# Decay products of a two-block layer kernel in one pass over stacked high and low parts, with their loads after x

## The reference

```python
h = rmsnorm(x, norm_mix[l])
proj = h @ w_in[l]
q, k, v, r, lr_f, lr_b, u, g_a, g_b = jnp.split(proj, split_points, axis=-1)
log_a_f = log_sigmoid(lr_f @ w_decay_up_fwd[l] + b_decay_fwd[l]) / 16
log_a_b = log_sigmoid(lr_b @ w_decay_up_bwd[l] + b_decay_bwd[l]) / 16
...
b = jnp.cumsum(log_a, axis=chunk)     # inside gla_chunked, chunks of 64 tokens
```

## Time and profile before

| | us |
|---|---|
| median of 3 runs | 1387.95 (1386.64 to 1388.97) |
| the profiled execution, its own time | 1387.89 |
| its span, from the first instruction to the last | 1385.6 |
| PE busy | 1334.7 (96% of the span) |
| DVE, ACT, POOL busy | 742.9, 574.2, 517.9 |
| mean granted TensorE clock | 0.992 of full speed |

### The profile page before, as it was taken

The page is one execution under the profiler, slowest core; times in us unless marked ns, Lnnn a source line. Parts: engine busy times, 40 slices in busy tenths (PEclk is TensorE's granted clock), DMA queues, the critical chain, the costliest instruction groups (busy, mean ns, idle before and its releaser), DMA issues.

```text
span 1385.6 us, 21045 instructions
## 1 busy us (share of the span) xinstructions
PE 1334.7 (96%) x8106; PEld 1093.6 (79%) x8106; DVE 742.9 (54%) x1226; ACT 574.2 (41%) x776; POOL 517.9 (37%) x130
## 2 busy tenths in 40 slices
PE   6999999999999999999999989999999999999997
PEld 4878889778887888888887867777878878787885
DVE  4642450664556888888822252334667777302553
ACT  6544353443343222222232245555554565533233
POOL 5332423333333333344344412323443343334331
PEclk9999999999999999999999999999999999999998
DMA  6232312215234455555423433231223222223221
GB/s 186 65 106 68 91 46 75 91 48 182 91 92 112 133 147 146 142 142 138 114 84 87 120 92 91 76 106 49 74 61 86 65 61 74 79 91 98 85 91 61
DMA packets 201731, 133.22 MB, mean 96 GB/s; under 512 B 4599, under 2 KB 197864, under 8 KB 201686
## 3 DMA queue, kind: packets, MB, share of 16 engines
q1 hardware_dynamic: 200390, 130.29, 32.1%
q10 hardware_dynamic: 848, 1.60, 0.4%
q0 software_dynamic: 448, 0.71, 0.2%
HBM read 130.46 MB, written 2.12 MB: 96 GB/s over the span
## 4 chain that ended last, share of the span: by engine, by line
issue 66%; POOL 16%; PE 15%; ACT 1%; DVE 1%; DMA 1%; POOLq 0%; SPq 0%; ACTq 0%
POOL wlo L447 15%; PE acc L469 4%; PE acc L471 4%; PE acc L470 4%; PE acc L1791 1%; PE acc L1793 1%; PE acc L1792 1%; DMA xnat<-in_x_dram 1%; ACT whi L443 0%; ACT hhi L692 0%; PE mid L2237 0%; POOLq L1764 0%; DVE hw L1607 0%; DVE wlo L1506 0%; DVE hw L1608 0%
## 5 line engine op out<-in xcount | busy, mean ns | idle before, releaser
L447 POOL TENSOR_TENSOR wlo<-raw,whi 128x2048 fp32r<-128x2048 f32 (+1 forms) x109 | 504.9, 4632 | 829.4 <-ACT whi L443 829.4
L469 PE MATMUL acc<-hhi,whi 128*128 128x512 f32 x1104 | 441.7, 400 | 4.4 <-DVE hq L1573 2.1
L471 PE MATMUL acc<-hhi,wlo 128*128 128x512 f32 x1104 | 431.5, 391 | 0.0
L470 PE MATMUL acc<-hlo,whi 128*128 128x512 f32 x1104 | 431.4, 391 | 0.0
L469 PEld LDWEIGHTS acc<-hhi,whi 128*128 128x128 f32 x1104 | 208.1, 188 | 51.1 <-issue 7.9
L470 PEld LDWEIGHTS acc<-hlo,whi 128*128 128x128 f32 x1104 | 208.2, 189 | 44.8 <-issue 3.4
L471 PEld LDWEIGHTS acc<-hhi,wlo 128*128 128x128 f32 x1104 | 208.0, 188 | 44.2
L443 ACT ACTIVATE whi<-raw 128x2048 fp32r<-128x2048 f32 (+1 forms) x110 | 203.5, 1850 | 48.7 <-PE acc L471 42.7
L1433 DVE TENSOR_TENSOR ada<-ada 128x512 f32<-128x512 f32 x24 | 108.9, 4538 | 0.8
L469 PE MATMUL acc<-ahi,whi 128*128 128x512 f32 x176 | 69.5, 395 | 1.8 <-POOL wlo L447 1.5
L875 ACT ACTIVATE fsg<-fsg 128x512 f32<-128x512 f32 x22 | 13.9, 632 | 138.2 <-DVE fsg L1447 138.1
(11 more groups left out here) (375 smaller groups left out, 2058.6 us busy)
## 6 DMA issues: line engine op xcount, KB each, us to landing
raw<-in_w_in_dram SPq DMA_DIRECT2D x56, 512.0 KB
raw<-in_w_in_dram SPq DMA_DIRECT2D x26, 1024.0 KB
raw<-in_w_ffn_in_dram SPq DMA_DIRECT2D x44, 512.0 KB
ada<-in_w_ada_dram SPq DMA_DIRECT2D x24, 512.0 KB, 3.8
raw<-in_w_ffn_out_dram SPq DMA_DIRECT2D x16, 704.0 KB
raw<-in_w_out_dram SPq DMA_DIRECT2D x8, 1024.0 KB
xnat<-in_x_dram SPq DMA_DIRECT2D x8, 512.0 KB, 7.1
raw<-in_w_branch_gla_dram SPq DMA_DIRECT2D x4, 1024.0 KB
```

Source lines behind the costliest of these rows:

```text
L447: nc.gpsimd.tensor_tensor(wlo[:, slot, 0:n], raw[:, slot, 0:n], whi[:, slot, 0:n].bitcast(f32), ALU.subtract).then_inc(s_unit_lo, 1)
L469: nc.tensor.matmul(acc[bank][:, :], h, xh[:, k, :], start=(k == 0), stop=False)
L470: nc.tensor.matmul(acc[bank][:, :], h, xl[:, k, :], start=False, stop=False)
L471: last = nc.tensor.matmul(acc[bank][:, :], lo, xh[:, k, :], start=False, stop=(k == nk - 1))
```

## The change

The four strips of `lrT` are summed and spread over all strips by one float32 product with a constant 0/1 matrix (`lr_sum`, a new input of 64 KB, loaded by SP behind `wlr`) into the bank M[0]. ACT copies that, rounded, to `lr3`; on strip 1 DVE replaces the copy by the low part (M[0] minus the rounded value). POOL copies `wup` rounded to `wup3` and replaces strip 2 by the low part of the weights; strip 3 of the weights stays zero, and only three copies of the up weights are loaded. One fp32r product of `wup3` with `lr3` then adds high x high (strip 0), high weights x low lr (strip 1) and low weights x high lr (strip 2). The eight decay products use it in place of the float32 product.

On POOL the wait for the last quarter of x moves ahead of all its loads, and the up weights come first, then `relb` and `hot`, the masks and `edge`; behind them stand a wait for the six loads and the two preparing operations, and only then `split_lo` of unit 1.

```diff
+    strip_sum = np.tile(np.eye(LR, dtype=f), (P // LR, P // LR))
...
             sp.dma_start(wlr[:, :, :], kview(w_in, C_LR, LR)).then_inc(s_lr_in, 16)
+            sp.dma_start(lr_sum[:, :], inp["strip_sum"]).then_inc(s_lr_in, 16)
...
             A(lrT[:, :], acc[b][:, :], ACT.Copy).then_inc(s_acc_free[b], 1)
+            act.wait_ge(s_lr3, 1)
+            A(lr3[:, :], M[0][:, :], ACT.Copy).then_inc(s_lr3, 1)
             act.wait_ge(s_col_mm, 2)
...
+            dve.wait_ge(s_lr3, 2)
+            V.tensor_tensor(lr3[LR:2 * LR, :], M[0][LR:2 * LR, :], lr3[LR:2 * LR, :].bitcast(f32), ALU.subtract)\
+                .then_inc(s_lr3, 1)
             dve.wait_ge(s_cols, 2)
...
+            pool.wait_ge(s_pool_prep, 3)
+            pool.wait_ge(s_x_in[TT - 1], 16)
+            for c in range(3):
+                pool.dma_start(wup[c * LR:c * LR + RANK, 0, :], inp["w_decay_up_fwd"][0]).then_inc(s_wup_in, 16)
+                pool.dma_start(wup[c * LR + RANK:(c + 1) * LR, 1, :], inp["w_decay_up_bwd"][0]).then_inc(s_wup_in, 16)
             pool.dma_start(relb[0:N_BUCKETS, :], inp["rel_bias_2"]).then_inc(s_bias_src, 16)
             pool.dma_start(hot[:, :], inp["hot"]).then_inc(s_bias_src, 16)
-            for c in range(P // LR):
-                pool.dma_start(wup[c * LR:c * LR + RANK, 0, :], inp["w_decay_up_fwd"][0]).then_inc(s_wup_in, 16)
-                pool.dma_start(wup[c * LR + RANK:(c + 1) * LR, 1, :], inp["w_decay_up_bwd"][0]).then_inc(s_wup_in, 16)
-            pool.wait_ge(s_x_in[TT - 1], 16)
...
+            pool.wait_ge(s_wup_in, 6 * 16)
+            nc.gpsimd.tensor_copy(wup3[:, :, :], wup[:, :, :]).then_inc(s_pool_prep, 1)
+            pool.wait_ge(s_pool_prep, 4)
+            lows = slice(2 * LR, 3 * LR)
+            nc.gpsimd.tensor_tensor(wup3[lows, :, :], wup[lows, :, :], wup3[lows, :, :].bitcast(f32), ALU.subtract)\
+                .then_inc(s_pool_prep, 1)
+            pool.wait_ge(s_pool_prep, 5)
             split_lo(pool, 1, 0)
...
             last.then_inc(s_acc_full, 1)
+            pe.wait_ge(*moved(U_LR, 0))
+            mm(M[0][:, :], lr_sum[:, :], lrT[:, :], start=True, stop=True).then_inc(s_lr3, 1)
             pe.wait_ge(s_rows_in, 12 * 16)
...
-            pe.wait_ge(*moved(U_LR, 0))
-            pe.wait_ge(s_wup_in, 2 * (P // LR) * 16)
+            pe.wait_ge(s_pool_prep, 5)
+            pe.wait_ge(s_lr3, 3)
...
-                mm(M[i % 4][:, :], wup[:, i // 4, (i % 4) * P:(i % 4 + 1) * P], lrT[:, :], start=True, stop=True)\
+                mm(M[i % 4][:, :], wup3[:, i // 4, (i % 4) * P:(i % 4 + 1) * P], lr3[:, :], start=True, stop=True)\
```

More of the change, by code:

```diff
@@ L108, in shape_constants @@
     hot[N_BUCKETS] = np.where(count > 0, np.log(np.maximum(count, 1)), NEG_INF)
-    return {"ident": ident, "masks": masks, "edge": edge, "hot": hot}
+    strip_sum = np.tile(np.eye(LR, dtype=f), (P // LR, P // LR))
+    return {"strip_sum": strip_sum, "ident": ident, "masks": masks, "edge": edge, "hot": hot}
 def build(nc, inp, out):
@@ L174, in build @@
     lrT = at("lrT", A0 + 44, [P, L])
+    lr_sum = at("lr_sum", A0 + 59, [P, P])
+    lr3 = at("lr3", A0 + 60, [P, L], f32r)
+    wup3 = at("wup3", A0 + 62, [P, 2, L], f32r)
     gq, gk = at("gq", A0 + 32, [P, L]), at("gk", A0 + 34, [P, L])
@@ L341, in build @@
         s_lr_in = sem("lr_in")
+        s_lr3 = sem("lr3")
         s_mask_src = sem("mask_src")
@@ L383, in build @@
         s_upad_zero = sem("upad_zero")
-        s_vrow_zero = sem("vrow_zero")
+        s_pool_prep = sem("pool_prep")
         s_wup_in = sem("wup_in")
@@ L557, in _ @@
             sp.dma_start(wlr[:, :, :], kview(w_in, C_LR, LR)).then_inc(s_lr_in, 16)
-            sp.wait_ge(s_vrow_zero, 3)
+            sp.dma_start(lr_sum[:, :], inp["strip_sum"]).then_inc(s_lr_in, 16)
+            sp.wait_ge(s_pool_prep, 3)
             for name, r in ROWS:
@@ L1734, in _ @@
         def _(pool):
[L1735 to L1739, removed]
+            nc.gpsimd.memset(vrow[:, :], 0.0).then_inc(s_pool_prep, 1)
+            nc.gpsimd.memset(wup[:, :, :], 0.0).then_inc(s_pool_prep, 1)
+            nc.gpsimd.memset(relb[:, :], 1.0).then_inc(s_pool_prep, 1)
+            pool.wait_ge(s_pool_prep, 3)
[3 more added lines that the diff above has]
+                pool.dma_start(wup[c * LR + RANK:(c + 1) * LR, 1, :], inp["w_decay_up_bwd"][0]).then_inc(s_wup_in, 16)
             pool.dma_start(relb[0:N_BUCKETS, :], inp["rel_bias_2"]).then_inc(s_bias_src, 16)
             pool.dma_start(hot[:, :], inp["hot"]).then_inc(s_bias_src, 16)
-            for c in range(P // LR):
-                pool.dma_start(wup[c * LR:c * LR + RANK, 0, :], inp["w_decay_up_fwd"][0]).then_inc(s_wup_in, 16)
-                pool.dma_start(wup[c * LR + RANK:(c + 1) * LR, 1, :], inp["w_decay_up_bwd"][0]).then_inc(s_wup_in, 16)
-            pool.wait_ge(s_x_in[TT - 1], 16)
             pool.dma_start(mask_src[:, :, :], inp["masks"]).then_inc(s_mask_src, 16)
@@ L1836, in _ @@
                         last.then_inc(s_xT, 1)
-            pe.wait_ge(s_lr_in, 16)
+            pe.wait_ge(s_lr_in, 32)
             b, _, _ = TL(U_LR, 0)
```

## The result

| | before | after |
|---|---|---|
| median of the runs side by side | 1387.95 us | 1393.66 us |
| lowest to highest (11 runs each) | 1385.96 to 1391.69 | 1388.15 to 1396.66 |
| profiled execution | 1387.89 | 1393.50 |
| its span | 1385.6 | 1391.0 |

The ratio is 1.0039, 95% interval 1.003 to 1.0049: the changed kernel is slower, by 5.4 us (the medians lie 5.7 apart). I had forecast 1389.4 and a range that ended at 1391.4. In the profiles the gap is 5.4 as well, and it has two parts: 0.7 us that are there when the start of the kernel is over, and almost 5 that come between 960 and 1030 us, nearly a millisecond behind the last line that the change touches.

The account below looks back on a forecast made before the run. PE, busy 96% of the span, was taken as the bound, its start settled by the DVE, ACT, POOL chain until 66.69 us. +0.5 (D, the fourth subtraction's end) + 1.0 (handover) = +1.5 on 1387.9 gave 1389.4, range 1386.4 to 1391.4.

Parts of the forecast that it names:

- x earlier: Start of kernel, loads of x: fourth square up to 1.5 us earlier; lr products' end -1.2 (bounds -1.5 and 0).
- The sum over strips: Lr products' end to high part of unit 2: 3.75 us, before 2.07; chain 1.7 longer, with earlier x D +0.5.
- the first item: The step on x coming earlier, taken as -1.2 us for the end of the lr products.
- POOL's preparation: POOL ahead of split 1: cast near 18.2 for 0.9 to 1.9 us, subtraction 2.3, split ending 26.7; added wait covered.
- One pass: Decay products on PE: eight cost 1.8 us, not 6.3; PE idles before product 7, perhaps half clock; gain 0.
- The sixth Abs and the handover: Abs waits for subtraction 4 alone; POOL's split of unit 3 goes ahead of the sixth running sum: +1.0 us.
- The sum at 67 us: PE's wait for the split of unit 4: +0.5 (D) + 1.0 (handover) = +1.5 us, now at 68.2.
- The step that failed: Behind 66.69 us PE's own progress sets everything going; gains or losses by then are kept, traces run in parallel.
- my rivals: No handover 1388.4 (0.25); shorter chain 1386.3 to 1387.3 (0.12); x no earlier 1389.6 to 1390.6 (0.08); slower 1391 and more (0.10).
- The slower one: Rival, 1391 and more, chance 0.10: POOL's preparation late (1391.4), or a half-clock stretch behind 68.2 (+1.7, 1391.1).

Follow-up runs that it names:

- e7: Kernel after with two waits on POOL: split of unit 3 behind the sixth running sum, split of unit 82 behind DVE's fourteen products; 1390.74 us, ratio 1.0018.
- e14: Kernel before plus two needless float32 products in PE's pause at 951.4 us; 1387.95 us, ratio 1.0002.
- e16: Kernel after, SP's weight load of unit 84 also waiting for the score products of the fifth level; 1390.95 us, ratio 1.0019.
- e17: Kernel after plus three tiny needless 8-column products in PE's pause at 952 us, moving the code behind them; 1390.75 us, ratio 1.0022.
- e18: Kernel before plus a needless 1 MB memory-to-memory load at about 971 us; 1389.77 us, ratio 1.0009.
- e3: Kernel before with only POOL's loads moved behind x, float32 decay products kept; 1385.66 us, ratio 0.9991.
- e11: e3 plus a wait on POOL holding the split of unit 82 until DVE's fourteen products are done; 1386.34 us, ratio 0.9992 to the kernel before.
- e12: e11 plus three needless float32 products in PE's pause ahead of the lr products; 1384.05 us, ratio 0.9976 to the kernel before.
- e13: Kernel after plus three needless float32 products in PE's pause ahead of the lr products; 1389.39 us, ratio 1.0011.
- e10: e7 plus two needless ACT copies ahead of the sigmoid, before PE's release near 67 us; 1390.97 us, ratio 1.0033.
- e8: Kernel after plus three needless ACT copies (1.5 us) ahead of the sigmoid; 1396.26 us, ratio 1.0061.
- e9: Kernel before plus four needless ACT copies (2.0 us) ahead of the sigmoid; 1391.51 us, ratio 1.0031.
- e5: Kernel after with POOL's loads ahead of x again, so the one pass alone; 1394.74 us, ratio 1.0045 to the kernel before.
- e4: Kernel before plus one needless ACT copy ahead of the sigmoid; 1388.06 us, ratio 1.0008.
- e15: e14 plus a wait on POOL holding the split of unit 82 until DVE's 14 products are through; 1387.85 us, ratio 1.0001.

## Why the prediction was wrong

*x earlier: right, the size too small.* The last square starts at 9.85, forecast 10.10; the lr products end at 22.02, 1.85 us earlier, where I took 1.2 with a bound of 1.5. The last square itself came 1.76 earlier (11.61 less 9.85), past the bound: ACT's own pace is 1.61 us a quarter here and not 1.72.

*The sum over strips: right.* From the copy to lrT to the high part of unit 2 it is 3.74 us (25.76 less 22.02), forecast 3.72 (3.75 behind the products' end, the copy 0.03 behind it). The fourth subtraction ends at 41.39, 0.13 earlier than before, where I had +0.5, by the first item alone.

*POOL's preparation: right.* The cast starts at 18.88 (18.2) and takes 1.04 us (0.9 to 1.9), the subtraction 2.34 (2.3), and split 1 ends at 26.96 (26.7). It was covered.

*One pass: right.* Four products in 1.35 us, PE idle for 2.19 ahead of product 7, then a stretch at half clock, all hidden.

*The sixth Abs and the handover: right in mechanism, mis-sized.* The Abs waits for the subtraction alone; POOL comes at 46.35, during the sixth subtraction, and goes ahead of the running sum, which takes 5.54 us. This is as "SBUF — State Buffer" of the Trainium skill (section "SBUF: two separate sides", on the shared port pair) has it: whichever starts first keeps the pair. But the price was 0.8 by the profile (the subtraction ends 0.13 earlier, and PE is released 0.66 later) where I took 1.0, and of that e7 gave back only 0.3.

*The sum at 67 us:* +0.66, forecast +1.5, bounds wide enough. Had the sentence behind it been true, the time would have been 1388.6, well inside the range.

*The step that failed* is that sentence: "behind it everything is set going by PE's own progress, so what PE gains or loses by 66.69 it keeps", and with it "Behind that point the two traces should run in parallel". They ran in parallel for 880 us. PE's progress is not the only thing that carries the start of the kernel further. Two others do: where the clock's slow stretches fall, and where PE's blocks of instructions end. The change altered both. The first moved POOL's split of unit 82 by 1.1 us against DVE's products (e14 shows that link by itself), the second put the request for a block behind the weights that the split sets going (e16, e17, e18). None of my rivals had either. The slower one was about POOL's preparation, where there was no trouble, and a half-clock stretch right behind 68.2, where there is none (granted clock 1.00 from 70 to 80 us).

*What stays open.* By the medians, which come from different rounds, e16 and e17 take back 2.7 to 2.9 us of 5.7 (2.8 and 2.3 of 5.4 by the ratios), about what the longer pause cost. About 0.7 is the late release. Some 2 us of the medians are left; slow stretches vary with the execution (half clock behind 1007 in e16 and e17, not in the kernel after), and no run isolates them. Nor is it settled why the stretch at 955 follows in the kernel before and not in the one after: both pause for 2.15 us there. PE's code alone does not decide it: e3 and e11 differ by nothing ahead of unit 82, and the profile of e3 has the stretch (0.66 of the clock from 953 to 958) and that of e11 has not (1.00). With one profile of each kernel it is not known how often each course is taken; one run of the kernel after took 1388.15 us, the median of the kernel before. In e12, e13 and e10 the clock does not fall under the lr products and the stretch at 955 is there, but other kernels have both, so a link with the first 25 us is a guess; e8 shows that a delay is not a simple handle on it.

## What to carry to other kernels

A pause that the profile puts down to "issue", in the middle of many small instructions, is to be laid beside the instruction rows of the DMA view: it may be a block of code that waits behind a bulk load, and then adding or removing instructions anywhere ahead of it, or issuing that load a few us later, changes the time. Before calling an engine's progress the only clock of the rest of a kernel, look for places where another engine asks for a shared port, or a load goes out, within some tenths of a us of a rival: these are the points where a shift of 1 us turns into 5. And an edit that saves time on an engine with slack should be timed one half at a time: here the loads behind x gained, and the one pass lost more.

## What the runs showed of the hardware

At the score products PE went on 1.2 to 1.5 us after the block of its instructions had been read, in the profiles of all 19 kernels (1.40 before, 1.48 after, 1.20 in e12, 1.50 in e9). Where the block did not come behind other transfers the whole pause was 0.5 us (111 products ahead of it, e12), 1.1 to 1.4 (113), 1.4 to 1.9 (117) and 1.8 to 2.2 (123); behind 0.65 to 1 MB of them it was 3.4 to 4.4. POOL, asking for the port amid DVE products that follow each other without a gap, got it when it came 1.2 us into them (kernel after, e5, e8, e9, e14, e16, e17) and was held off until the last one when it came 2.3 us into them (kernel before, e3, e4, e13, e18); I have no rule for that. A slow stretch of TensorE's clock need not cost anything where it falls: the one at 955 us, taken away alone, brought no time at all (e15).
